# A transformer layer on Trainium2: the first FFN layer by Strassen's method for 14 of its 16 feature pairs

## The reference

```python
h = x * (1.0 + sc2) + sh2
f = jnp.square(jax.nn.relu(h @ w_ff1[l])) @ w_ff2[l]
x = layer_norm(ALPHA * x + gt2 * f, ln2_g[l], ln2_b[l])
```

## Time and profile before

| | us |
|---|---|
| median of 3 runs | 919.72 |
| the profiled execution, its own time | 917.63 |
| its span, first to last instruction | 915.8 |
| TensorE busy | 876.0 (96%) |
| VectorE busy | 360.9 (39%) |
| ScalarE busy | 176.7 (19%) |
| GpSimd busy | 90.9 (10%) |
| granted TensorE clock, mean | 0.992 |

### The profile page before, as it was taken

How to read it: one execution, slowest core, us unless ns; L and a number is a source line. 1 busy time by engine, 2 the same in 40 slices (tenths; PEclk the granted TensorE clock), 3 DMA queues, 4 the chain that set the end, 5 groups by cost and what they waited for, 6 DMA issues and landing times.

```text
span 915.8 us, 11949 instructions
## 1 busy us (share of the span) xinstructions
PE 876.0 (96%) x4900; PEld 543.7 (59%) x4900; DVE 360.9 (39%) x834; ACT 176.7 (19%) x364; POOL 90.9 (10%) x90
## 2 busy tenths in 40 slices
PE   6999899999999999999999999999999999999984
PEld 3446756766667764688878878577455333333331
DVE  5646816433223338464276311662255111101014
ACT  4126612100000000421341211350021111101001
POOL 0045303301011110300000000000020000000000
PEclk9999999999999999999999999999999999999999
DMA  9998857543334446034253123102988999999993
GB/s 371 430 420 307 325 233 299 207 183 150 129 129 161 193 193 240 1 103 172 92 200 151 31 82 111 74 8 92 379 355 299 371 403 425 418 423 422 420 414 121
DMA packets 24669, 218.40 MB, mean 238 GB/s; under 512 B 3657, under 2 KB 3937, under 8 KB 10018
## 3 DMA queue, kind: packets, MB, share of 16 engines
q1 hardware_dynamic: 21330, 205.76, 56.4%
q0 software_dynamic: 3280, 11.82, 3.5%
HBM read 218.75 MB, written 2.10 MB: 241 GB/s over the span
## 4 chain that ended last, share of the span: by engine, by line
PE 79%; DVE 7%; DMA 6%; SPq 3%; ACT 2%; issue 2%; DVEq 0%; POOLq 0%; ACTq 0%
PE psum L2402 12%; PE psum L2424 9%; PE psum L524 8%; PE psum L477 6%; PE psum L1428 6%; PE psum L2190 4%; DMA scr<-in_gates 4%; PE psum L2383 3%; PE psum L2162 3%; PE psum L786 3%; PE psum L1483 3%; PE psum L1452 3%; DMA ring<-in_stream 2%; PE psum L2134 2%; PE psum L604 2%
## 5 line engine op out<-in xcount | busy, mean ns | idle before, releaser
L2402 PE MATMUL psum<-hT,ring 128*128 128x256 f32 x512 | 115.4, 379 | 1.1 <-issue 1.1
L2402 PEld LDWEIGHTS psum<-hT,ring 128*128 128x128 f32 x512 | 97.1, 190 | 26.7 <-issue 14.2
L524 PE MATMUL psum<-hT,ring 128*128 128x272 f32 (+2 forms) x320 | 72.7, 388 | 0.0
L524 PEld LDWEIGHTS psum<-hT,ring 128*128 128x128 f32 x320 | 60.6, 190 | 11.3 <-issue 0.4
L477 PE MATMUL psum<-hT,ring 128*128 128x256 f32 x256 | 59.8, 391 | 0.0
L2424 PE MATMUL psum<-scr 128*128 128x512 f32 x128 | 59.5, 592 | 0.0
L2863 DVE TENSOR_TENSOR scr<-ring 128x512 f32<-128x512 f32 x16 | 11.1, 692 | 121.6 <-PE psum L2424 121.6
L1428 PE MATMUL psum<-ring,hT 128*32 128x512 f32 (+1 forms) x240 | 56.7, 594 | 2.1 <-DMA scr<-in_gates 2.0
L2190 PE MATMUL psum<-ring,hT 128*128 128x512 f32 (+1 forms) x128 | 53.1, 574 | 2.2 <-ACT hT L2495 2.1
L477 PEld LDWEIGHTS psum<-hT,ring 128*128 128x128 f32 x256 | 48.9, 194 | 7.3 <-issue 0.2
L1428 PE MATMUL psum<-scr,hT 128*64 128x512 f32 (+1 forms) x192 | 51.8, 615 | 1.1 <-issue 1.1
(11 more groups left out here) (562 smaller groups left out, 1252.1 us busy)
## 6 DMA issues: line engine op xcount, KB each, us to landing
ring<-in_stream SPq DMA_DIRECT2D x54, 2048.0 KB, 10.2
ring<-in_gates SPq DMA_DIRECT2D x9, 2048.0 KB, 22.7
ring<-in_downs SPq DMA_DIRECT2D x14, 1024.0 KB, 21.1
scr<-in_gates SPq DMA_DIRECT2D x6, 2048.0 KB, 26.0
scr<-in_gates SPq DMA_DIRECT2D x8, 1024.0 KB, 25.1
scr<-in_downs SPq DMA_DIRECT2D x8, 1024.0 KB, 15.9
scr<-in_stream SPq DMA_DIRECT2D x3, 2048.0 KB, 18.9
rowB<-in_rows POOLq DMA_DIRECT2D x5, 1024.0 KB, 12.2
```

The lines of the kernel that those rows point to most:

```text
L524: last = mm(psum[:, g % 4, cols], w[:, k, m * P:(m + 1) * P], hT[:, k, cols], start=(k == 0), stop=(k == KD - 1))
L2402: last = mm(psum[:, f if f < 4 else 0, 0:NT], w[:, k, m * P:(m + 1) * P], hT[:, k, META:L2], start=(k == 0), stop=(k == KD - 1))
```

## The change

The tiles of chunk 0 stay as they are. The 28 tiles of chunks 1 to 7 are made as 14 pairs, q = 2 to 15, by Strassen's method too. The 2x2 blocks are: k even and odd (the weights' rows), the two tiles of the pair (the weights' columns), and the two halves of the tokens. Each of the seven products has four matmuls of 128x128 by 128 columns, 28 matmuls for a pair in place of 16 of 256 columns. They go to bank 0, in four regions of 128 columns, in two parts: `ff1_first(q)` makes products 1, 4, 5, 6 (16 matmuls) and `ff1_second(q)` 2, 3, 7 (12 matmuls).

VectorE gets new work: once, four sums of halves of the tokens (`ff1_token_sums`, into `rowB[:, 0]`); per pair four sums of weight blocks of 128x512 (into `rowB[:, 1]`), and the combination of the products (`ff1_take_first`, `ff1_take_second`), which Relu did not need before. ScalarE now does Relu in two pieces, GpSimd squares a pair's two tiles one after the other. As `rowB` is taken, both loads of rows move behind the last square. Some semaphores are shared to free names (`att_a`, `att_v`); each such wait stands for the same event as before.

```diff
+        FT_ = rowB[:, 0, :, :].rearrange("p a (b k n) -> p (a b) k n", k=KD // 2, n=P)
+        FS_ = rowB[:, 1, :, :].rearrange("p a (b k n) -> p (a b) k n", k=KD // 2, n=P)
+        fp1 = gnB[:, 0, 0:P]
+        fmix = gnB[:, 0, P:4 * P].rearrange("p (a n) -> p a n", n=P)
...
@@ gpsimd
-            rows(2, 0, S.in_row0)
...
             affine(1, 2)
-            pool.wait_ge(S.affine, 2)
+            for f in range(4):
+                pool.wait_ge(S.ff_rl, f + 1)
+                nc.gpsimd.tensor_tensor(fTr[:, f, :], frl[:, f, :], frl[:, f, :], ALU.mult).then_inc(S.ff_sq, 1)
+            for q in range(2, FT // 2):
+                pool.wait_ge(S.ff_rl, 2 * q + 2)
+                if q >= 8:
+                    pool.wait_ge(S.y2_mm, q - 7)
+                for f in range(2):
+                    pair = frl[:, 2 * (q % 2) + f, :]
+                    nc.gpsimd.tensor_tensor(fTr[:, (2 * q + f) % 16, :], pair, pair, ALU.mult).then_inc(S.ff_sq, 1)
+            rows(2, 0, S.in_row0)
             rows(3, 1, S.in_row1)
...
@@ tensor
+            def ff1_product(q, i):
+                w = ring_at(ff1_chunk(q // 2)).rearrange("p (k a m f) -> p a m k f", a=2, m=4, f=P)
+                m = 2 * (q % 2)
+                region = {1: 0, 2: 0, 6: 1, 7: 1, 4: 2, 5: 3, 3: 3}[i]
+                for k in range(KD // 2):
+                    lhsT, rhs = {1: (w[:, 0, m, k], hT[:, 2 * k, tok(0)]),
+                                 2: (w[:, 1, m, k], hT[:, 2 * k + 1, tok(0)]),
+                                 3: (FS_[:, 3, k], hT[:, 2 * k + 1, tok(1)]),
+                                 4: (w[:, 1, m + 1, k], FT_[:, 3, k]),
+                                 5: (FS_[:, 0, k], FT_[:, 0, k]),
+                                 6: (FS_[:, 1, k], FT_[:, 1, k]),
+                                 7: (FS_[:, 2, k], FT_[:, 2, k])}[i]
+                    last = mm(psum[:, 0, region * P:(region + 1) * P], lhsT, rhs, start=(i == 1 and k == 0),
+                              stop=(i in (2, 7, 4, 3) and k == KD // 2 - 1), skip_group_check=True)
+                return last
+            def ff1_first(q):
+                if q % 2 == 0:
+                    landed_wait(pe, ff1_chunk(q // 2))
+                pe.wait_ge(S.ff_rl, 1 if q == 2 else 2 * q - 1)
+                if q > 2:
+                    pe.wait_ge(S.ff_c, q - 2)
+                ff1_product(q, 1)
+                pe.wait_ge(S.ff_s, 2 * (q - 2) + 1)
+                ff1_product(q, 4)
+                ff1_product(q, 5)
+                ff1_product(q, 6).then_inc(S.ff_a, 1)
+            def ff1_second(q):
+                pe.wait_ge(S.ff_p, q - 1)
+                pe.wait_ge(S.ff_s, 2 * (q - 2) + 2)
+                last = ff1_product(q, 2)
+                if q % 2:
+                    last.then_inc(S.used, 1)
+                ff1_product(q, 3)
+                ff1_product(q, 7).then_inc(S.ff_b, 1)
...
             for c in range(1, 8):
                 whole = c < 5
-                ff1(4 * c)
+                ff1_first(2 * c)
                 ff2(2 * c - 2, (5, 6, 1))
-                ff1(4 * c + 1)
+                ff1_second(2 * c)
                 ff2(2 * c - 2, (2, 3, 7, 4) if whole else (2, 3)).then_inc(S.y2_mm, 1)
-                ff1(4 * c + 2)
-                ff2(2 * c - 1, (5, 1))
-                ff1(4 * c + 3)
-                ff2(2 * c - 1, (2, 3)).then_inc(S.used, 1)
+                ff1_first(2 * c + 1)
+                ff2(2 * c - 1, (5, 1, 2))
+                ff1_second(2 * c + 1)
+                ff2(2 * c - 1, (3,)).then_inc(S.used, 1)
                 ff2(2 * c - 1, (6, 7, 4) if whole else (6,)).then_inc(S.y2_mm, 1)
...
@@ scalar
+            for q in range(2, FT // 2):
+                act.wait_ge(S.ff_b, q - 1)
+                act.wait_ge(S.ff_sq, 2 * q - 2)
+                nc.scalar.activation(frl[:, 2 * (q % 2), 0:P], psum[:, 0, 0:P], ACT.Relu).then_inc(S.ff_rl, 1)
+                act.wait_ge(S.ff_c, q - 1)
+                rest = arena(4096 + 512 * (q % 2) + P, 3 * P)
+                nc.scalar.activation(rest, rest, ACT.Relu).then_inc(S.ff_rl, 1)
...
@@ vector
+            def ff1_sums_first(q):
+                if q % 2 == 0:
+                    landed_wait(dve, ff1_chunk(q // 2))
+                a11, a12, a21, a22 = ff1_weights(q)
+                link(v.tensor_tensor(FS_[:, 0], a21, a22, ALU.add))
+                v.tensor_tensor(FS_[:, 1], FS_[:, 0], a11, ALU.subtract).then_inc(S.ff_s, 1)
+            def ff1_sums_second(q):
+                a11, a12, a21, a22 = ff1_weights(q)
+                v.tensor_tensor(FS_[:, 2], a11, a21, ALU.subtract)
+                dve.wait_ge(S.ff_s, 2 * (q - 2) + 1)
+                v.tensor_tensor(FS_[:, 3], a12, FS_[:, 1], ALU.subtract).then_inc(S.ff_s, 1)
+            def ff1_take_first(q):
+                regions = psum[:, 0, :].rearrange("p (a n) -> p a n", n=P)
+                dve.wait_ge(S.ff_a, q - 1)
+                link(v.tensor_copy(fp1, regions[:, 0]))
+                v.tensor_tensor(fmix, fp1.unsqueeze(1).broadcast_to([P, 3, P]), regions[:, 1:4], ALU.add)\
+                    .then_inc(S.ff_p, 1)
+            def ff1_take_second(q):
+                regions = psum[:, 0, :].rearrange("p (a n) -> p a n", n=P)
+                dve.wait_ge(S.ff_b, q - 1)
+                dve.wait_ge(S.ff_rl, 2 * q + 1)
+                dve.wait_ge(S.ff_p, q - 1)
+                dve.wait_ge(S.ff_sq, 2 * q - 2)
+                f = 2 * (q % 2)
+                v.tensor_tensor(frl[:, f, P:NT], fmix[:, 0], regions[:, 3], ALU.add)
+                v.tensor_tensor(frl[:, f + 1, :].rearrange("p (a n) -> p a n", n=P), fmix[:, 1:3],
+                                regions[:, 1:2].broadcast_to([P, 2, P]), ALU.add).then_inc(S.ff_c, 1)
...
-            weight_sums(0)
-            for j in range(FT // 2):
-                token_sums(j)
-                if j + 1 < FT // 2:
-                    weight_sums(j + 1)
+            ff1_token_sums()
+            dve.wait_ge(S.affine, 2)
+            ff1_sums_first(2)
+            ff1_sums_second(2)
+            weight_sums(0)
+            token_sums(0)
+            for q in range(2, FT // 2):
+                ff1_take_first(q)
+                if q + 1 < FT // 2:
+                    ff1_sums_first(q + 1)
+                ff1_take_second(q)
+                if q + 1 < FT // 2:
+                    ff1_sums_second(q + 1)
+                weight_sums(q - 1)
+                token_sums(q - 1)
+            weight_sums(FT // 2 - 1)
+            token_sums(FT // 2 - 1)
```

More of the change, by code:

```diff
@@ L99, with ff1_chunk @@
 ADA_BANK = {4: 1, 5: 2, 6: 3, 7: 2, 8: 3, 9: 0, 10: 4, 11: 5}
+def ff1_chunk(c):
+    return AT["ffn"] + (0 if c == 0 else 2 * c - 1)
 def ada_chunk(c):
@@ L203, in build @@
             gram ab rd_mm rd_v rd_a u_mm uv landed8 s_mm sv vn_mm vn_v o_mm o_v os orv on on_tr
-            mod_ev flag sel xg xgv sct yv yh idx hrow xr0 landed9 perm entries
+            mod_ev ff_a ff_b ff_p ff_c ff_s flag sel xg xgv sct yv yh idx hrow xr0 landed9 perm entries att_a att_v
             """.split()
@@ L2325, in _ @@
             last.then_inc(S.sc, 1)
[L2327 removed]
+            pe.wait_ge(S.att_a, 5)
             ada(5)
@@ L2403, in ff1 @@
                               start=(k == 0), stop=(k == KD - 1))
-                last.then_inc(S.used if m == 3 else S.ff_mm, 1)
+                last.then_inc(S.used if f == 3 else S.ff_mm, 1)
+            def ff1_product(q, i):
[13 more added lines that the diff above has]
+                return last
@@ L2529, in _ @@
                                             bias=V("be", k, k + 1), scale=V("ge", k, k + 1))
-            last.then_inc(S.meta_h, 1)
+            last.then_inc(S.att_a, 1)
             act.wait_ge(S.used, AT["head"] + KD)
@@ L2579, in _ @@
             act_hT(2)
-            for f in range(FT):
-                if f % 4 < 3:
-                    act.wait_ge(S.ff_mm, 3 * (f // 4) + f % 4 + 1)
-                else:
-                    c = f // 4
-                    act.wait_ge(S.used, AT["ffn"] + (0 if c == 0 else 2 * c - 1) + 1)
-                if f >= 4:
-                    act.wait_ge(S.ff_sq, f - 3)
-                nc.scalar.activation(frl[:, f % 4, :], psum[:, f if f < 4 else 0, 0:NT], ACT.Relu).then_inc(S.ff_rl, 1)
-                if f == 3:
-                    act.wait_ge(S.gt_mm, 2)
-                    nc.scalar.copy(gtB[:, 1, :], psum[:, 4:6, :].rearrange("p a b -> p (a b)")).then_inc(S.gtB, 1)
+            for f in range(4):
+                if f < 3:
+                    act.wait_ge(S.ff_mm, f + 1)
+                else:
+                    act.wait_ge(S.used, ff1_chunk(0) + 1)
+                nc.scalar.activation(frl[:, f, :], psum[:, f, 0:NT], ACT.Relu).then_inc(S.ff_rl, 1)
+            act.wait_ge(S.gt_mm, 2)
+            nc.scalar.copy(gtB[:, 1, :], psum[:, 4:6, :].rearrange("p a b -> p (a b)")).then_inc(S.gtB, 1)
+            for q in range(2, FT // 2):
[5 more added lines that the diff above has]
```

(3 more changed lines are left out.)

77 lines of the change are left out of this document (40 added, 37 removed).

## The result

The changed kernel takes **927.85 us** (median of 4 runs, 926.36 to 930.11) beside 919.15 us for the kernel before on the same chip (4 runs, 918.04 to 920.28): a ratio of 1.0105, 95% interval 1.0087 to 1.0124 (here and below the ratio is reckoned with its interval from the single runs, and can differ from the quotient of the two medians by about 0.001; here the latter is 1.0095). It is slower, by 8.7 us. The forecast was 922, range 915 to 929, with 0.50 on slower. The profiled execution took 926.36 us, span 924.2, so 8.4 more in the span than before.

The account below looks back on a forecast made before the run. The prediction took PE alone to bound the first FFN layer, with VectorE newly late: -9.1 + 7.2 + 4.1 + 0.2 = +2.4 us, 920.0 from the profiled execution, hence 922 as median, range 918.5 to 925.5 (wider 915 to 929).

Parts of the forecast that it names:

- One of the prediction's own signs of being wrong: First FFN layer: the forecast would be wrong if PE's waits stood already in chunks 1 to 4.
- PE's shorter work, 14 pairs: PE's ff1: 56 records of 0.112 us, 6.27 a pair instead of 6.92, so 9.1 us less for 14 pairs.
- chunks 5 to 7, 5 rounds: Ahead of ff2, q = 10 to 14: PE waits 1.44 us for VectorE five times, 7.2 us.
- rows: Before VectorE's first output operation: ln2's rows land 7.8 us after issue, 0.2 us late.
- the round of 6.73 us: VectorE's work from PE's end of ff1_second(q) until ff2(q-1) may start: 6.13 us undisturbed plus 0.6 for two squares.
- the rival in which GpSimd holds VectorE for longer: In every round, GpSimd holds VectorE for the whole square, 1.22 us a pair: +8.9, 928.6 us; chance 0.13.
- That row: VectorE's L2865, 0.99 us instead of 0.69 beside GpSimd; source of the 0.30 us a square taken as most alike.
- the 12.2 of the rival: Rival for ln2's row loads: they land late, after 12.2 us, adding 4.6 us, 926.5; chance 0.12.
- The 0.30 us set aside for the issue of the row loads: After q = 15: GpSimd's issue of the row loads delays VectorE by 0.30 us, making 5.51 into 5.81.
- VectorE is never late: Rival for the sums of a pair: VectorE's round shortens by 1.44 us, total -6.2, 913.5 us; chance 0.09.
- squares cost nothing: Rival for GpSimd's squares: they fall between VectorE's operations, total -1.5, 918.2 us; chance 0.15.
- weight loads show: Rival for PE's 128-column records: weight loads make them 0.145 us each, +16.8, in all +23, 942.7 us; chance 0.04.

Follow-up runs that it names:

- Experiment 1: The changed kernel with the 28 squares of pairs 2 to 15 on ScalarE instead of GpSimd: 922.61 us, ratio 1.0044.
- experiment 8: The changed kernel with four matmuls of 512 columns keeping PE busy in its wait before ff2(14): 927.37 us, ratio 1.0098.
- Experiments 2 to 4: Changed kernel, weight_sums before ff1_take_second: 918.54 us; kernel before, only row loads moved late: 926.67; changed kernel, weight_sums earlier and row wait at first use: 911.74.
- experiment 3: The kernel before with only the two row loads moved behind the last square: 926.67 us, ratio 1.0094.
- experiment 6: Changed kernel with weight_sums earlier, row wait at first use, squares on ScalarE, token_sums(14) ahead of ff1_take_second(15): 910.28 us, ratio 0.9912.
- experiment 7: Changed kernel, weight_sums and token_sums(14) earlier, row wait at first use, squares on ScalarE, two matmuls before the second layer's first projection: 909.78 us, ratio 0.9907.

## Why the prediction was right, and where its sizes were off

The direction and the mechanism came out: PE's 128-column records run at half the price, VectorE ends last, and PE waits ahead of `ff2` in chunks 5 to 7 and after the last chunk, nowhere inside `ff1`. One of the prediction's own signs of being wrong came too: PE is held up already in chunks 1 to 4, by 0.15 us a round. And the size didn't come out: +8.7 instead of +2.4. By the prediction's terms, in us, from the two profiles:

| term | forecast | measured |
|---|---|---|
| PE's shorter work, 14 pairs | -9.1 | -9.4 (6.25 a pair, not 6.27) |
| chunks 1 to 4, 8 rounds | 0 | +1.2 (12.41 - 12.26 = 0.15 each) |
| chunks 5 to 7, 5 rounds | +7.2 | +9.3 (12.41 - 10.54 = 1.87 each) |
| last wait | +4.1 | +3.9 |
| lower clock after that wait | none | +1.7 |
| rows | +0.2 | +0.7 (1.45 - 0.80) |
| sum | +2.4 | +7.4 |

The marks agree nearly: PE reaches the second layer's transposes at 373.26 instead of 365.46, 7.8 later. L506 adds 1.7 at the lower clock, 540 to 560 us gives as much back (there the kernel before has its slow stretch), and 0.6 us in the rest of the span and 0.3 outside it stay unassigned.

- **The step that failed most is the round of 6.73 us.** It measured 7.08. Of the difference 0.22 is the collision, 0.41 a square instead of 0.30, and 0.11 the passing on to PE, 0.15 instead of 0.04. Both are small, but the slack in chunks 1 to 4 was 0.27, and the round's lateness counts 13 times. The prediction named the alternative: the rival in which GpSimd holds VectorE for longer decides from 0.44 a square. The truth lies close under it, in the range of 0.30 to 0.45 that the rows gave; I took its lower end, from a single row. Experiment 1 shows the size: without squares 0.80 instead of 1.62 a round.
- **That row was not the one most alike.** L2865 is the third of the weight sums, which waits for the second (its `s_dve`), while the squares of a round meet the first and the second. After the last chunk they meet the third and fourth:

```profile
343.75 2.06 POOL L2131 TENSOR_TENSOR scr<-scr 128x256 f32<-128x256 f32 x2 [10.35 <-ACT scr L2641]
344.36 0.98 DVE L2915 TENSOR_TENSOR scr<-ring,scr 128x512 f32<-128x512 f32 x1
345.38 0.98 DVE L2916 TENSOR_TENSOR scr<-ring,scr 128x512 f32<-128x512 f32 x1
...
346.28 0.28 DVE L2922 TENSOR_TENSOR scr<-scr 128x128 f32<-128x128 f32 x1
```

  Here the starts are 1.02 and 0.90 apart instead of 0.73 and 0.60: 0.29 and 0.30 a square, the forecast's price. Experiment 1 confirms it, the last wait falls by 0.58 and the others by 0.82. The likely reason, not tested: between a sum and one that waits for it VectorE is free for 0.12 us anyway (starts 0.72 apart instead of 0.60), and the square uses that.
- How they collide can be read from the round shown: from 281.73 to 284.37 lie the last 0.49 us of L2953's turn (until L2913 starts at 282.22), two squares and two sums. Undisturbed they would add up to 0.49 + 2 x 0.61 + 0.60 + 0.72 = 3.03 us; the stretch is 2.64. The Trainium skill ("SBUF — State Buffer", SBUF: two separate sides) calls the shared port pair an exclusive lock for the whole instruction. The trace agrees as far as the two take turns and each square lasts 1.03 us; but a square shuts VectorE out for 0.41 to 0.42 us, not for its whole 0.61.
- **The rows, and the clock, of which nothing was said.** The rows landed 10.06 us after their issue, between the 7.8 taken and the 12.2 of the rival, so 13.9 behind the mark instead of 11.4. A wait of 3.7 us was priced at its length; behind it PE's products took 1.7 us longer at the lower clock. The two terms of the table can't be charged apart: in experiment 8 the products are fast again, PE waits 3.17 us instead of 1.45 further on, and the time stays. So the term that was too small is that of the rows, 0.2 forecast and 1.7 + 0.7 = 2.4 found, and the lower clock costs nothing more here, since it runs while the rows are late.
- The cost of the rows was this small only because PE was itself late. Experiments 2 to 4 show what the forecast didn't see: with PE on time the same load costs 7 to 9 us, and any repair of the sums would have run into it. The 0.30 us set aside for the issue of the row loads didn't come: the sums beside it (L2922 above) take 0.28 us, as always.
- "VectorE is never late" and "squares cost nothing" fall by the trace; "weight loads show" falls by the pace of 0.1116.

What the measurement of 927.85 comes near is the rival's 928.6, in part by chance: its waits (17.8) are above those measured (14.4), and the late rows with the lower clock, which it left out or priced too low, make up for some.

## What to carry to other kernels

An engine that becomes the last one should do what depends on nothing new before the event that the others wait for; one moved call, `weight_sums`, was worth 9 us here, and made the difference between a change that loses 1% and one that can win. When a change takes over a buffer and so moves a load behind it, move the wait to the load's first use as well, and price it as if the other lateness were already mended: costs that hide behind one another show only one at a time. Where the slack is smaller than the spread of the rows behind a cost, look for what separates the rows before one is taken; here it was whether the disturbed sum waits for the one before it.

## What the runs showed of the hardware

- VectorE and GpSimd in turns on short operations: a sum of 128x512 takes 1.10 us instead of 0.69, one of 128x128 0.70 instead of 0.28, a square of 128x256 1.03 instead of 0.61. The extra is 0.41 to 0.42 for sums of either size that wait for nothing, and 0.29 to 0.30 for the third and fourth weight sum in the last round (0.98 instead of 0.69).
- The granted clock fell to its lower level (0.55 on the mean of 2.5 us) behind a wait of PE of 3.7 us, and in experiment 3 (0.50) with one of 7.0 us; with PE kept busy in the first of these places it stayed at 1.00 there (experiment 8). It is also at its lower level behind waits of 0.86 and 1.69 us in experiment 6, but not behind 0.80 and 1.69 in the kernel before. Why it comes at 540 to 560 us in the kernel before and in experiment 7, where PE is busy throughout, stays open.
- Matmuls of 128 rows by 128 columns follow one another at 0.1116 us a record with a new weight load each, 3% over half of the 0.2163 for 256 columns.
- A row load of 1 MB landed after 7.8 us in the kernel before, after 10.1 in the changed kernel, and after 13.4 in experiment 3. Ring loads were under way each time, with the DMA engines 61% to 80% busy in the first case and nearly all of the time (some 420 GB/s) in the other two.
